# Retention gates as four more units of half-size products, ahead of queries and keys, with the modulation slabs moved forward

## What is computed

```python
p = split_parts(h_lat @ w_in, ODD_PARTS)      # q 1024, k 1024, v 2048, g 2048 columns
pc = project_parts(h_ctx, w_in, ODD_PARTS, ['k', 'v'])
...
o_fw, _ = retention_chunked(q_l, k_l, v_l, log_g_fw, s_fw)
o_bw, _ = retention_chunked(flip(q_l), flip(k_l), flip(v_l), log_g_bw, s_bw)
y_lat = gated_head_norm(o_fw + flip(o_bw), p['g']).astype(dt) @ w_out

def gated_head_norm(o, g_raw, gain=None):
    y = rms_norm(from_heads(o), gain) * jax.nn.silu(g_raw...)
```

## Time and profile before

| | value |
|---|---|
| median of three runs | 2661.12 us (2659.16 to 2667.38) |
| the profiled execution | 2661.45 us |
| its span in the trace | 2659.6 us |
| PE busy | 2562.7 us, 96% |
| DVE busy | 1508.7 us, 57% |
| ACT busy | 646.7 us, 24% |
| bytes moved by DMA | 386.59 MB, mean 145 GB/s |

### The profile page before, as it was taken

How to read it: one execution, slowest core, us unless ns; L and a number is a source line. 1 busy time by engine, 2 the same in 40 slices (tenths; PEclk the granted TensorE clock), 3 DMA queues, 4 the chain that set the end, 5 groups by cost and what they waited for, 6 DMA issues and landing times.

```text
span 2659.6 us, 38231 instructions
## 1 busy us (share of the span) xinstructions
PE 2562.7 (96%) x15612; PEld 1937.7 (73%) x15612; DVE 1508.7 (57%) x2965; ACT 646.7 (24%) x1705; POOL 0.2 (0%) x4
## 2 busy tenths in 40 slices
PE   6999899999999999999999999999999999999999
PEld 2545557888887864589996845658997864667999
DVE  4856667655876543126663654426773664433785
ACT  3145412111002110212202152233321134232320
POOL 0000000000000000000000000000000000000000
PEclk9999999999999999999999999999999999999999
DMA  8522115555574684245653432125664333114563
GB/s 338 202 81 49 40 32 162 156 176 171 200 275 160 258 303 164 79 127 150 174 171 135 143 90 96 65 95 143 169 189 139 137 117 95 65 65 139 164 177 124
DMA packets 335210, 386.59 MB, mean 145 GB/s; under 512 B 11052, under 2 KB 264124, under 8 KB 322748
## 3 DMA queue, kind: packets, MB, share of 16 engines
q1 hardware_dynamic: 332300, 378.15, 44.2%
q10 hardware_dynamic: 2736, 6.01, 0.6%
HBM read 383.08 MB, written 1.05 MB: 144 GB/s over the span
## 4 chain that ended last, share of the span: by engine, by line
PE 80%; DVE 9%; issue 4%; DMA 4%; ACT 3%; ACTq 0%; SPq 0%; DVEq 0%
PE acc L833 26%; PE acc L884 11%; PE acc L872 10%; PE mx L833 10%; PE acc L898 6%; PE acc L914 2%; DMA mod_w<-in_w_ada 2%; PE acc L1196 2%; PE acc L1145 2%; PE mx L1544 1%; DVE arena L2417 1%; DVE arena L3216 1%; PE mx L1006 1%; ACT hT L1762 1%; DVE hT L2450 1%
## 5 line engine op out<-in xcount | busy, mean ns | idle before, releaser
L833 PE MATMUL acc<-arena 128*128 128x128 f32 (+1 forms) x2184 | 353.1, 304 | 3.6 <-DVE arena L2965 1.0
L833 PEld LDWEIGHTS acc<-arena 128*128 128x128 f32 x2184 | 306.7, 191 | 22.3 <-ACT gate L2100 1.4
L884 PE MATMUL acc<-hT,ring 128*128 128x256 f32 (+1 forms) x1280 | 305.5, 401 | 2.2 <-ACT hT L1762 1.3
L884 PEld LDWEIGHTS acc<-hT,ring 128*128 128x128 f32 x1280 | 242.5, 190 | 63.3 <-issue 32.1
L2417 DVE SCALAR_TENSOR_TENSOR arena<-mod_w,vcols,arena 128x2048 f32<-128x2048 f32 x98 | 228.4, 2348 | 70.3 <-DMA mod_w<-in_w_ada 58.0
L872 PE MATMUL acc<-ring,hT 128*128 128x512 f32 x576 | 249.5, 593 | 5.9 <-ACT hT L1852 4.6
L898 PE MATMUL acc<-ring,hT 128*128 128x512 f32 x512 | 247.6, 605 | 0.7 <-ACT hT L1883 0.7
L872 PEld LDWEIGHTS acc<-ring,hT 128*128 128x128 f32 x576 | 108.7, 190 | 143.3 <-issue 137.7
L2781 DVE TENSOR_TENSOR arena<-ring 128x512 f32<-128x512 f32 (+1 forms) x136 | 91.8, 675 | 197.3 <-PE acc L833 182.3
L833 PE MATMUL acc<-hT,ring 128*128 128x128 f32 (+1 forms) x1208 | 187.0, 304 | 4.7 <-ACT hT L1852 2.2
L833 PE MATMUL acc<-arena,ring 128*128 128x128 f32 (+1 forms) x1160 | 182.9, 300 | 3.5 <-DVE arena L2832 1.8
(11 more groups left out here) (427 smaller groups left out, 3405.3 us busy)
## 6 DMA issues: line engine op xcount, KB each, us to landing
ring<-in_w_in SPq DMA_DIRECT2D x28, 2048.0 KB
mod_w<-in_w_ada SPq DMA_DIRECT2D x48, 1024.0 KB, 5.4
ring<-in_ffn_w_in SPq DMA_DIRECT2D x88, 512.0 KB
ring<-in_w_up SPq DMA_DIRECT2D x88, 512.0 KB
mod_w<-in_mod_w SPq DMA_DIRECT2D x40, 1024.0 KB, 5.0
ring<-in_odd_w_in SPq DMA_DIRECT2D x12, 2048.0 KB
ring<-in_ffn_w_out SPq DMA_DIRECT2D x16, 1024.0 KB
ring<-in_w_down SPq DMA_DIRECT2D x16, 1024.0 KB
```

The lines of the kernel that those rows point to most:

```text
L833: ins = nc.tensor.matmul(out, w[:, k, :], h[:, k, :], start=start and k == 0, stop=stop and k == n - 1, skip_group_check=more)
L884: ins = nc.tensor.matmul(b[:, 0:hi - lo], w[:, k, P * f:P * (f + 1)], hT[:, k, lo:hi], start=k == 0, stop=k == KD - 1)
```

## The change

Four units are added for the gates: chunks 4 to 7, latent tokens only (`RV_UNITS`). They follow the eight units of the values in the same pipeline; their corners are written without an activation, and ACT applies Silu to them in place after the keys. The input sums of pair 1 move from the arena into `gate`, since their place is now the gates' output, and the two decay tables that are loaded into `gate` are issued after the units. SP loads the gates' weights ahead of those of queries and keys. Of the 28 slabs, DVE takes three in each of the units 1 to 7 (two before), one in each of the units 8 to 11, and three after; `MOD_SUM_AFTER` and `slab_tile` follow.

```diff
-MOD_SUM_AFTER = {"even": (13,), "odd": (4, 8, 19, 30)}
+MOD_SUM_AFTER = {"even": (13,), "odd": (3, 5, 8, 18)}
-MOD_UNITS, MOD_ODD = (0, 2, 2, 2, 2, 2, 2, 2), (8, 2, 2, 2)
+MOD_UNITS, MOD_ODD = (0, 3, 3, 3, 3, 3, 3, 3, 1, 1, 1, 1), 3
...
+RV_UNITS = [(c, pair) for c in range(4) for pair in range(2)] + [(c, 1) for c in range(4, 8)]
+def rv_last(c):
+    return max(q for q in range(len(RV_UNITS)) if RV_UNITS[q][0] == c) + 1
...
-    for c in range(4):
-        a.ring_used("unit", 2 * c + 2, 2)
-    tiles("odd", (("ret_q", [4, 4]), ("ret_k", [4, 4]), ("ret_g", [2] * 4)))
-    a.slab_tile += [a.tile["ret_v"] + n for n in (2, 2, 2, 2, 4, 4, 4, 4, 6, 6, 6, 6, 8, 8, 8, 8, 8, 10, 10, 10, 10, 10,
-                                                  12, 12, 14, 14, 16, 16)]
+    for c in range(8):
+        a.ring_used("unit", rv_last(c), 2)
+    tiles("odd", (("ret_q", [4, 4]), ("ret_k", [4, 4])))
+    a.slab_tile += [a.tile["ret_v"] + n for n in [2] * 6 + [4] * 6 + [6] * 6 + [8] * 3 + [10, 12, 14, 16, 16, 18, 18]]
...
         def rv_out(q, i, t):
 
-            return rv[:, 2 * (q % 2) + i, 512 * (q // 2) + 256 * t:512 * (q // 2) + 256 * t + 256]
+            c, pair = RV_UNITS[q]
+            at = 512 * (c % 4) + 256 * t
+            return rv[:, 2 * pair + i, at:at + 256] if c < 4 else rg[:, i, at:at + 256]
...
-            for c in (4, 5, 6, 7, 0, 1, 2, 3, 8, 9, 10, 11):
+            for c in (4, 5, 6, 7, 8, 9, 10, 11, 0, 1, 2, 3):
                 load(wcols(a["odd_w_in"][0], 512 * c, 512 * c + 512))
...
             for lo in (256, 256, 0, 0):
                 by_feature(4, lo, 512, where="odd")
-            for _ in range(4):
-                by_token(LAT, 512, where="odd")
...
             for c in range(4):
+                act.wait_ge(rv_c10, 9 + c)
                 for t in range(2):
-                    evac(rg[:, t, 512 * c:512 * (c + 1)], 512, ACT.Silu)
-                    mod_after("odd")
+                    g = rg[:, t, 512 * c:512 * (c + 1)]
+                    ins = nc.scalar.activation(g, g, ACT.Silu)
+            ins.then_inc(rg_silu, 1)
...
-                if q % 2 == 1 and q < 7:
-                    value_weights_summed(q // 2 + 1)
-                if q < 8:
+                if q < units - 1 and RV_UNITS[q + 1][0] > RV_UNITS[q][0]:
+                    value_weights_summed(RV_UNITS[q + 1][0])
+                if q < units:
...
+            mod_slabs(MOD_ODD)
             for h in range(RET):
-                mod_slabs(MOD_ODD[h])
...
-            job_done("ret_g", 8)
+            dve.wait_ge(rg_silu, 1)
             weighted(0)
```

More of the change, by code:

```diff
@@ L526, in rv_sums @@
         def rv_sums(pair):
-            return [view(8192 + 2048 * pair + 512 * j, 4, P) for j in range(4)]
+            if pair == 0:
+                return [view(8192 + 512 * j, 4, P) for j in range(4)]
+            return [gate[:, j // 2, 512 * (j % 2):512 * (j % 2) + 512].rearrange("p (k n) -> p k n", k=4) for j in range(4)]
         def rv_weight_sums(c):
@@ L1435, in retention_values @@
                 B = {}
-                units = 8
+                units = len(RV_UNITS)
                 def x_(q):
@@ L1444, in product1 @@
                 def product1(q):
-                    if q % 2 == 0:
+                    if RV_UNITS[q][0] not in B:
                         first = tile.n
                         weights(512)
-                        B[q // 2] = rv_tile(first)
+                        B[RV_UNITS[q][0]] = rv_tile(first)
                     if q >= 2:
                         pe.wait_ge(rv_c01, q - 1)
-                    product(x_(q), A[q % 2][0][0], B[q // 2][0][0], True, True,
+                    product(x_(q), A[RV_UNITS[q][1]][0][0], B[RV_UNITS[q][0]][0][0], True, True,
                             (lambda k: pe.wait_ge(h_ready, KD * use + k + 1)) if q == 0 else lambda k: None).then_inc(rv_p1, 1)
@@ L1455, in product2 @@
                     need(pe, rv_c00, q)
-                    product(seven(5, 256), A[q % 2][0][1], B[q // 2][1][0], True, True,
+                    product(seven(5, 256), A[RV_UNITS[q][1]][0][1], B[RV_UNITS[q][0]][1][0], True, True,
                             (lambda k: pe.wait_ge(h_ready, KD * use + KD // 2 + k + 1)) if q == 0
@@ L1460, in product5 @@
                 def product5(q):
-                    pe.wait_ge(rv_t, 4 * (q // 2) + 2)
+                    pe.wait_ge(rv_t, 4 * RV_UNITS[q][0] + 2)
                     if q < 2:
@@ L1465, in product5 @@
                         pe.wait_ge(rv_c10, q - 2)
-                    product(z_(q), rv_sums(q % 2)[0], B[q // 2][0][1], True, True)
+                    product(z_(q), rv_sums(RV_UNITS[q][1])[0], B[RV_UNITS[q][0]][0][1], True, True)
                 def product6(q):
-                    pe.wait_ge(rv_t, 4 * (q // 2) + 3)
+                    pe.wait_ge(rv_t, 4 * RV_UNITS[q][0] + 3)
                     if q < 2:
@@ L1472, in product6 @@
                     pe.wait_ge(rv_p1s, q + 1)
-                    product(x_(q), rv_sums(q % 2)[2], rv_weight_sums(q // 2)[1], False, True, more=True).then_inc(rv_p6, 1)
+                    product(x_(q), rv_sums(RV_UNITS[q][1])[2], rv_weight_sums(RV_UNITS[q][0])[1], False, True, more=True).then_inc(rv_p6, 1)
                 def product7(q):
                     pe.wait_ge(rv_u2s, q + 1)
-                    product(x_(q), rv_sums(q % 2)[1], rv_weight_sums(q // 2)[0], False, True, more=True).then_inc(rv_p7, 1)
+                    product(x_(q), rv_sums(RV_UNITS[q][1])[1], rv_weight_sums(RV_UNITS[q][0])[0], False, True, more=True).then_inc(rv_p7, 1)
                 def product4(q):
@@ L1482, in product4 @@
                     pe.wait_ge(rv_u3s, q + 1)
-                    product(x_(q), rv_sums(q % 2)[3], B[q // 2][1][1], False, True, more=True).then_inc(rv_x, 1)
+                    product(x_(q), rv_sums(RV_UNITS[q][1])[3], B[RV_UNITS[q][0]][1][1], False, True, more=True).then_inc(rv_x, 1)
                 def product3(q):
-                    pe.wait_ge(rv_t, 4 * (q // 2) + 4)
+                    pe.wait_ge(rv_t, 4 * RV_UNITS[q][0] + 4)
                     pe.wait_ge(rv_c11, q + 1)
-                    product(z_(q), A[q % 2][1][1], rv_weight_sums(q // 2)[2], False, True, more=True).then_inc(rv_z, 1)
+                    product(z_(q), A[RV_UNITS[q][1]][1][1], rv_weight_sums(RV_UNITS[q][0])[2], False, True, more=True).then_inc(rv_z, 1)
                 product1(0)
@@ L2151, in table @@
                 act.dma_start(r_D[:, h % 2], a["const_ret"][h]).then_inc(dtab_in[h % 2], 16)
-            table(0)
-            table(1)
             own.n = 0
             p1, u2, u3 = (rv_copies[:, j] for j in range(3))
-            for q in range(9):
+            units = len(RV_UNITS)
+            for q in range(units + 1):
                 b = q % 2
-                if q < 8:
+                if q < units:
                     act.wait_ge(rv_p1, q + 1)
@@ L2178, in _ @@
                     nc.scalar.activation(u3[:, b], seven(b, 256), ACT.Copy).then_inc(rv_u3s, 1)
+            table(0)
+            table(1)
             for f in range(8):
@@ L2958, in value_weights_summed @@
                 if 0 in only:
-                    need(dve, rv_z, 2 * c - 2)
+                    if c >= 2:
+                        dve.wait_ge(rv_z, rv_last(c - 2))
                     dve.wait_ge(w_in[t // 2 % RING], pl.landed[t][1])
@@ L2988, in _ @@
             p1, u2, u3 = (rv_copies[:, j] for j in range(3))
-            for q in range(10):
-                if 1 <= q < 9:
+            units = len(RV_UNITS)
+            for q in range(units + 2):
+                if 1 <= q < units + 1:
                     o = q - 1
```

4 lines of the change are left out of this document (1 added, 3 removed).

## The result

The changed kernel takes 2706.01 us (median of five runs, 2702.27 to 2706.59) against 2661.12: the ratio is 1.0166, with an interval of 1.0155 to 1.0177. It is slower by 1.7%, about 45 us, where 2707 was forecast. The profiled execution took 2704.46 us with a span of 2702.6, 43.0 us more than before, and PE's granted clock over the whole span was 0.988 of 2.4 GHz (before 0.996).

What follows compares the result with a forecast made beforehand. PE, busy for 96% of the span, was taken as the bound. The terms -6.6 - 3.8 + 42.5 + 8.1 + 2.6 + 2.8 = +45.6 us took the profiled 2661.45 us to 2707 us, range 2691 to 2720.

Steps and rivals of the forecast that it cites:

- gates' arithmetic: Eight gate jobs removed, 55.0 us, and four units of 12.09 us added, 48.4 us: a gain of 6.6 us.
- waits that existed: PE's old waits for DVE's corner ahead of product 3, 0.28 + 1.37 + 1.09 + 1.08 us: gain 3.8 us.
- third slab, four waits: Slabs 2, 8, 14, 20, issued behind weight tiles, hold up product 3 of units 1, 3, 5, 7: cost 42.5 us.
- clock: PE's granted clock falls after each of the four long waits, 2.0 us each: cost 8.1 us, bounds 0 and 13.4.
- gate tiles: In the gate units PE waits 1.0 us for chunk 6's tile and 1.6 for chunk 7's: cost 2.6 us.
- end of the stage: After the last key, without the gate jobs' cover, PE waits in the scores: cost 2.8 us, bounds 2.0 and 4.5.
- the landing L: Time from issue to landing of a slab behind a weight tile: 9.8, 11.1 or 11.3 us, mean 10.7.
- The even units: Units 2, 4 and 6, between the delayed ones: no wait ahead of product 3, with 1 us to spare.
- X: End of product 4 of unit 1, which releases chunk 2's tile; slab 2 is issued at X + 0.7.
- The rival of the full DMA: Slabs 4 and 5 come slower, so even units wait too, 1 to 4 us each: 2710 to 2719 us; chance 0.12.
- the first rival: DVE gets slabs 2, 8, 14 and 20 without holding up PE: 2656 us, no measurable change; chance 0.06.

Runs made afterwards that it cites:

- experiment 1: Changed kernel with two slabs in each of units 1 to 7, one per gate unit, ten after the units; 2663.72 us, ratio 1.0007.
- experiment 3: Changed kernel with only SP's list altered, slabs 2 and 3 issued ahead of chunk 2's tile, later pieces shifted by two; 2671.35 us, ratio 1.0028.
- the run with spare matmuls: Changed kernel with ten 128x512 matmuls into an unused bank ahead of product 3 of units 1, 3, 5 and 7; 2698.59 us, ratio 1.0136.
- experiments 2 and 5: 2: kernel before with only slabs moved, three per value unit, 2708.43 us; 5: changed kernel with only the end of the stage reordered, 2701.19 us.

## Why the prediction was right

The terms in the order of the prediction, what was forecast and what the runs show:

| term | forecast | found |
|---|---|---|
| gates' arithmetic | -6.6 | not taken alone |
| waits that existed | -3.8 | gone from the changed kernel |
| third slab, four waits | +42.5 | +38.6 |
| clock | +8.1 | +9.6 |
| gate tiles | +2.6 | +2.7 |
| end of the stage | +2.8 | +4.1 |
| sum | +45.6 | +44.6 with the first two as forecast; 43.0 by the spans |

The terms found add up to 1.6 us too much. By the distances of starts the waits that existed cost 4.3 us and not 3.8, and before the change the first score started 0.5 us late, on ACT's copy of a sum ([0.32 <-ACT modc L1788] at 1084.17), a wait that the prediction did not count and that is gone. The rest, 0.6 us, was not followed.

**The waits that existed.** The short waits ahead of product 3 are not there any more, as forecast. They are hidden by the long ones, not cured: experiment 1, without long waits, has 0.48, 0.46 and 1.31 us again.

**The four waits.** The mechanism is shown from both sides: moving the slabs alone makes the loss, and taking the slab out of its place behind the tile, by its number or by its order alone, takes the loss away (all of it in experiment 1, 33 of 39 us of the stretch in experiment 3). The sum of the four delays, 9.93 + 10.00 + 9.73 + 8.91 = 38.6 us, is just under my lower bound of 38.9. The step that was off is the landing L, for which I took the mean of three, 10.7 us; the changed kernel has 9.7 to 9.9 throughout, near the first of the three before. The last wait is shorter by 1.0 us, where I had 1.1, because its slab is the first of a group. Why the second and third landing before took 11.1 and 11.3 us was not settled.

**The clock.** The forecast of 8.1 us came from windows far away, and the run with spare matmuls shortens the stretch by 8.1 us. That match is luck. Beside the run with spares, product 3 takes 3.54, 3.68, 3.68 and 3.55 us in the changed kernel in place of 1.80 to 1.90, and what follows it is slow for another 0.4 to 0.9 us, 9.6 us in all. The run with spares gives 1.5 us of that back elsewhere: its four waits are 0.3 us longer together, and it waits 1.2 us more for gate tiles (from product 3(8) to 3(9) there are 15.35 us in place of 14.11), since the tile of chunk 6 takes 9.1 us from its issue to the first sum (990.30 to 999.43) and not 7.9. Why it does was not settled. So a fall costs 2.4 us here, where I had 2.0. Nor does the way of working it out carry over: a window's length times the missing share of the clock gives 14 x 0.37 = 5.2 us for each window with 0.63, 20.7 in all, because most of the slow time lies within the wait, where PE has nothing to run. The windows far away have a smaller missing share, and the two errors nearly cancel. "TensorE: Matmul & The Clock Gate" in the Trainium skill, section "HAM oscillation — how this bites in real kernels", describes a kernel in which a DMA wait between bursts sends the clock back to half, so that every burst starts cold. The trace agrees for all four waits (0.63 in each window).

**The even units.** None waits, as predicted. I had 1 us to spare; in unit 2 there are 3.2 us (DVE starts on the corner at 884.81, and PE's product 3(2) starts at 888.62), as slab 5 is done 1 us sooner after X than I had it and the slow clock brings PE there 1.2 us later. The rival of the full DMA falls with that: its share is 0.88 in the window of the wait, but 0.29 in the next unit.

**The gate tiles.** The tiles of chunks 6 and 7 land as forecast: the issue at 997.57 and the first sum at 1005.47 are 7.9 us apart, at 1011.68 and 1019.70 it is 8.0, where I took 8.0. From product 4(8) to 4(9) and on to 4(10) there are 14.1 and 14.2 us (forecast 14.1 and 14.1), which is 1.0 and 1.7 us more than the products, the sum and the turn take. PE's share of it in the timeline is in these rows:

```profile
1007.88 3.72 PE L842 MATMUL acc<-ring,gate 128*128 128x256 f32 x16 [0.47 <-DVE ring L2973]
...
1019.65 1.99 PE L842 MATMUL acc<-ring,hT 128*128 128x256 f32 x8 [0.71 <-DMA ring<-in_odd_w_in]
...
1022.12 1.99 PE L842 MATMUL mx<-ring,gate 128*128 128x256 f32 x8 [0.47 <-DVE ring L2973]
```

**The end of the stage.** The wait was predicted as 2.8 us and is 2.4 to 2.5. The mis-sized part is the clock behind it: head 1's 16 score records take 5.26 us in place of 3.62, so 1.6 us more, which I had only in the upper bound (4.5). ACT's eight Silus take 4.26 us, 0.53 each, where I had 0.6. They end at 1126.99 and DVE's turn at 1127.15, so it is the turn that holds up the weighting, by little, and not the Silus.

One step of the first rival was worked out wrongly: for four waits of 1.2 us slab 2 would have to land before X + 1.8, not X + 1. It landed at X + 10.5, so nothing hangs on it.

## What to carry to other kernels

When a load is used one step earlier, look at where it is issued, not only at whether the bytes fit: here 1 MB behind a 2 MB tile in the same queue is late by some 5 us, and since the tile itself waits for the product that stands two ahead of the one that wants the slab, another 6 us go before it is even issued; the engine stands still for 10 us each time. The list that orders the queue has to move with the use, and even then three slabs per unit cost six small waits in experiment 3. A gain in arithmetic (6.6 us) is easily given back by the placement that comes with it, so measure the two apart: edits of slab counts, lists and order alone turned a loss of 45 us into a gain of 7.

## What the hardware showed beyond that

A wait of the same length has the clock fall in one run and not in another. Ahead of head 1's scores PE waits 2.37 us in the changed kernel, and the records after it are slow (5.26 us, granted clock 0.88 in the window of 1122 to 1136); in the run with spares the same wait is followed by 5.38 us; in experiments 1 and 3 the same 2.37 us are followed by 3.69 us, at a granted clock of 1.00 in experiment 1:

```profile
1081.00:1095.00 14.00, 11.63 (x44) 7.99 (x43) 6.78 (x12) 6.03 (x10) 0.00 (x0) 1.00 0.48 152
```

A wait of 2.96 us in experiment 3 (at 893.15, then 1.96 us for the product) had no fall either, while one of 2.80 (at 956.60, then 3.67) had one. Nor is it plain at 3.7 us: such a wait stands near the start of every run, and the same 64 records behind it take 27.70 us in the kernel before and 29.40 in the changed one, with a granted clock of 1.00 and of 0.88 in the window of 42 to 56:

```profile
42.12 27.70 PE L872 MATMUL acc<-ring,hT 128*128 128x512 f32 x64 [3.67 <-ACT hT L1852]
41.94 29.40 PE L881 MATMUL acc<-ring,hT 128*128 128x512 f32 x64 [3.66 <-ACT hT L1859]
```

So between 2 and 3.7 us a wait's length alone does not tell whether the clock falls. In this layer all twelve waits of 8.75 us and above (in the changed kernel and in experiments 2 and 5) had a fall, and none had one where PE was given spare matmuls to run. The idle time of 14.5 us ahead of the program's first matmul is another matter: the granted clock there is given as 1.00.
